# Neighbourhood attention: the scores of two heads in two neighbouring rows as four 64x64 blocks in the quarters of TensorE's array

## The reference, cut to what matters

```python
def neighbourhood_attention(q, k, v, rpb):
    """q,k,v: (B, T, H, dh); rpb: (H, 2*NA_KH-1, 2*NA_KW-1). Returns (B, T, H*dh)."""
    B, T, H, dh = q.shape
    R = T // GRID_W
    W = GRID_W
    KH = min(NA_KH, R)
    KW = NA_KW
    grid = lambda t: t.reshape(B, R, W, H, dh).transpose(0, 3, 1, 2, 4)
    qg, kg, vg = grid(q), grid(k), grid(v)
    rows = jnp.arange(R)
    row_start = jnp.clip(rows - KH // 2, 0, R - KH)
    row_idx = row_start[:, None] + jnp.arange(KH)[None, :]
    k_rows = kg[:, :, row_idx]
    v_rows = vg[:, :, row_idx]
    scores = jnp.einsum('bhrqd,bhrikd->bhrqik', qg, k_rows).astype(jnp.float32)
    scores = scores * (dh ** -0.5)
    dr_idx = row_idx - rows[:, None] + (NA_KH - 1)
    cols = jnp.arange(W)
    dc = cols[None, :] - cols[:, None]
    dc_idx = jnp.clip(dc, -(KW - 1), KW - 1) + (KW - 1)
    bias = rpb.astype(jnp.float32)[:, dr_idx[:, None, :, None], dc_idx[None, :, None, :]]
    col_start = jnp.clip(cols - KW // 2, 0, W - KW)
    in_win = (cols[None, :] >= col_start[:, None]) & (cols[None, :] < col_start[:, None] + KW)
    scores = jnp.where(in_win[None, None, None, :, None, :], scores + bias[None], -jnp.inf)
    p = jax.nn.softmax(scores.reshape(B, H, R, W, KH * W), axis=-1).reshape(B, H, R, W, KH, W)
    out = jnp.einsum('bhrqik,bhrikd->bhrqd', p.astype(v.dtype), v_rows)
    return out.transpose(0, 2, 3, 1, 4).reshape(B, T, H * dh)
```

## Time and profile before

| what | us |
|---|---|
| runs: median of 3 | 3050.95 |
| runs: lowest, highest | 3050.57, 3057.44 |
| the profiled execution's own time | 3060.26 |
| its span, first to last instruction | 3058.5 |
| neighbourhood stage in it, from the barrier's end to the next stage's first product | 2019.0 to 2164.6 |

### The profile page before, as it was taken

One profiled execution on the slowest core, in us unless ns is written; L12 is line 12 of the kernel. 1 busy time (PEld: TensorE's weight loads), 2 busy tenths in 40 slices (PEclk: granted clock), 3 DMA queues, 4 the chain that ended last, 5 costly groups with the idle time before them and its releaser, 6 DMA issues.

```text
span 3058.5 us, 30798 instructions
## 1 busy us (share of the span) xinstructions
PE 2889.4 (94%) x12002; PEld 1718.3 (56%) x12002; DVE 1169.8 (38%) x1999; ACT 629.4 (21%) x1351; POOL 724.3 (24%) x552
## 2 busy tenths in 40 slices
PE   7999998888988999999879999999999999999998
PEld 5886544888446666666534455557544444444443
DVE  6715766566122111111143135456543314133142
ACT  4001232222221222211222211157230000000001
POOL 3213556543111000000021000146521122111220
PEclk9999999999998999999989999999999999999999
DMA  8734494000237999999661100030201101111001
GB/s 265 224 54 52 96 228 136 1 28 29 107 143 282 397 424 428 426 426 395 250 231 55 56 0 15 14 107 1 90 31 52 55 28 41 42 55 47 36 28 55
DMA packets 180120, 415.12 MB, mean 136 GB/s; under 512 B 30644, under 2 KB 103796, under 8 KB 170872
## 3 DMA queue, kind: packets, MB, share of 16 engines
...
...
## 4 chain that ended last, share of the span: by engine, by line
PE 86%; DVE 6%; DMA 3%; issue 2%; ACT 1%; POOL 1%; SPq 0%; ACTq 0%; POOLq 0%; DVEq 0%
PE bank L3788 27%; PE bank L2554 9%; PE bank L2557 8%; PE bank L2984 5%; PE bank L1266 4%; PE bank L748 4%; PE bank L1946 4%; PE bank L3158 3%; PE bank L232 3%; PE bank L3497 2%; PE bank L3156 2%; PE bank L883 2%; PE bank L3487 2%; PE bank L1844 1%; PE bank L1841 1%
## 5 line engine op out<-in xcount | busy, mean ns | idle before, releaser
L3788 PE MATMUL bank<-w_ff,uT 128*128 128x512 f32 x640 | 276.0, 592 | 0.0
L3788 PE MATMUL bank<-hT,w_ff 128*128 128x512 f32 x512 | 225.1, 598 | 4.3 <-DVE hT L3591 4.3
L3788 PEld LDWEIGHTS bank<-w_ff,uT 128*128 128x128 f32 x640 | 121.7, 190 | 153.0 <-issue 153.0
L3911 DVE TENSOR_TENSOR x_out<-x_out,bank 128x512 f32<-128x512 f32 x140 | 94.5, 685 | 291.7 <-PE bank L3788 291.6
L2554 PE MATMUL bank<-e_w,e_xsT 128*128 128x256 f32 x832 | 184.4, 383 | 1.6 <-DVE e_xsT L2640 1.6
L2557 PE MATMUL bank<-e_w,e_xsT 128*64 128x256 f32 x1408 | 161.0, 389 | 17.1 <-issue 16.9
L2554 PEld LDWEIGHTS bank<-e_w,e_xsT 128*128 128x128 f32 x832 | 158.3, 191 | 32.5 <-issue 11.3
L2984 PE MATMUL bank<-w_gla,nT 128*128 128x512 f32 x384 | 167.5, 596 | 3.0 <-DMA w_gla<-in_w_in 1.7
L3788 PEld LDWEIGHTS bank<-hT,w_ff 128*128 128x128 f32 x512 | 97.9, 192 | 126.7 <-issue 126.7
L3788 PE MATMUL bank<-h_sum,w_ff 128*128 128x512 f32 x384 | 166.1, 592 | 0.0
L2557 PEld LDWEIGHTS bank<-e_w,e_xsT 128*64 128x64 f32 x1408 | 114.3, 140 | 67.5 <-issue 28.6
...
...
## 6 DMA issues: line engine op xcount, KB each, us to landing
...
w_ff<-in_w_ff SPq DMA_DIRECT2D x32, 1024.0 KB, 5.2
...
```

The costliest lines, as they stand in the source:

```text
L3788: t = pe.matmul(bank[:, :], still, moving, start=step in (0, 1, 3) and f == 0, stop=f == 3, skip_group_check=True)
L3911: v.tensor_tensor(dst, dst, k.bank[4 * ((ph + step) % 2) + g][:, :], ALU.add).then_inc(*s.added.up().inc)
```

## The change

The scores of one pair of heads are made for two neighbouring grid rows at once, 2r and 2r + 1, as four products of 64 features by 64 queries by 512 keys (`near_scores_tensor`, L3498). The features' half of the partitions picks the half of the array's rows; the half of the partitions that the output is written to picks the half of its columns. For the even row head 0's queries go to partitions 0 to 63 and head 1's to 64 to 127, for the odd row the other way round (`near_head`). So the four products lie in the four quarters of the array. Each row's scores are in a bank of their own, as before: banks p and p + 4 for the pair p.

For the odd row the heads stand turned, so the bias table is needed a second time with its halves swapped: `near.bias[1]`, loaded by two transfers of 64 partitions each behind the other transfers of that queue. VectorE waits for it ahead of its first instruction of the stage. It lies where the gated linear attention keeps a table, so its transfers wait until that one's last readers are done (`sums_made`).

The diagonal matrices go, with their copies and clears; the queries are scaled as ScalarE copies the projection. The transposed weights are written over the scores in `n_sc` instead of to `n_pT`, so the next reduce of a bank waits for the value products (`av_made`) instead of the transposes. The generators' order is by pairs (`NEAR_ORDER`: 0, 4, 1, 5, 2, 6, 3, 7), with other pauses.

The loads of SyncE's queue at the end of the projections, before and now. `n_bias` is the bias table, `w_ff` the weights of the next stage.

```diff
@@ -3067,7 +3067,7 @@
        "state_ready o_taken o_squared eps_added o_root o_ready o_turned mix_out zeroed")
 PAIRS = NAH // 2
 NEAR_RATE = 1.8
-Near = namedtuple("Near", "qkT val_even val_odd bias q2 sc pT st")
+Near = namedtuple("Near", "qkT val_even val_odd bias sc st")
 
 
...
@@ -3081,11 +3081,11 @@
 def gla(k, mix_s, mix_b, decay_s, decay_b, bias_rows, near):
 
     s = [k.on(GLA, way="_fwd"), k.on(GLA, way="_bwd")]
-    d = k.on("unit_made unit_out", "wv_got wqk_0 wqk_1 val_odd_got bias_got", way="_near")
+    d = k.on("unit_made unit_out", "wv_got wqk_0 wqk_1 val_odd_got bias_got bias_turned_got", way="_near")
...
-    near_loads(k, mix_s, d, wv, wqk, near, bias_rows)
+    near_loads(k, mix_s, s, d, wv, wqk, near, bias_rows)
...
@@ -3112,8 +3111,8 @@
 
     n_sets = lambda name, at, n, size: [k.at(f"n_{name}{j}", at + j * size * 4, P, size) for j in range(n)]
     return Near(k.at("n_qkT", U_AT + 48 * KB, P, 2 * PAIRS, T), k.at("n_val_even", U_AT + 80 * KB, P, NT, BANK), k.at("n_val_odd", N_AT, P, NT, BANK),
-                k.at("n_bias", N_AT + 16 * KB, P, PAIRS, (2 * KH - 1) * W), n_sets("q2", EARLY_AT, NSETS, P), n_sets("sc", U_AT + 96 * KB, NSETS, KH * W),
-                n_sets("pT", U_AT + 112 * KB, NSETS, KH * W), n_sets("st", EARLY_AT + 4 * KB, NSETS, 8))
+                [k.at(f"n_bias{j}", at, P, PAIRS, (2 * KH - 1) * W) for j, at in enumerate((N_AT + 16 * KB, U_AT + 96 * KB))],
+                n_sets("sc", U_AT + 112 * KB, NSETS, KH * W), n_sets("st", EARLY_AT + 4 * KB, NSETS, 8))
 
 
 def near_unit_of(u):
...
@@ -3134,9 +3133,13 @@
         sy.dma_start(wqk[at % 2][:, :, :], cols).then_inc(*(d.wqk_0, d.wqk_1)[at % 2].up().inc)
     sy.wait_ge(*d.unit_made(NT + 4 * PAIRS))
     sy.wait_ge(*d.unit_out(NT))
-    sy.dma_start(near.bias[:, :, :], bias_rows).then_inc(*d.bias_got.up().inc)
+    sy.dma_start(near.bias[0][:, :, :], bias_rows).then_inc(*d.bias_got.up().inc)
...
+    for way in gla_s:
+        sy.wait_ge(*way.sums_made(NT))
+    for lo in (0, W):
+        sy.dma_start(near.bias[1][W - lo:P - lo, :, :], bias_rows[lo:lo + W, :, :]).then_inc(*d.bias_turned_got.up().inc)
 
 
 def near_units_tensor(k, d, nT, wv, wqk):
@@ -3170,15 +3173,7 @@
             yield
         a.wait_ge(*d.unit_made(u + 1))
         dst = near.val_even[:, m, :] if m is not None else near.qkT[:, c, h * BANK:(h + 1) * BANK]
-        a.activation(dst, k.bank[6 + u % 2][:, :], ACT.Copy).then_inc(*d.unit_out.up().inc)
-
-
-def near_ready(k, decay_s, near):
-
-    g = k.nc.gpsimd
-    g.wait_ge(*decay_s.la_ready(2))
-    for n in range(NSETS):
-        g.memset(near.q2[n][:, :], 0.0).then_inc(*k.G.up().inc)
+        a.activation(dst, k.bank[6 + u % 2][:, :], ACT.Copy, scale=NAD ** -0.5 if m is None and c < PAIRS else 1.0).then_inc(*d.unit_out.up().inc)
 
 
 def gla_halves(n):
@@ -3400,18 +3395,29 @@
 def neighbourhood(k, d, b):
 
     k.nc.vector.wait_ge(*d.bias_got(1))
-    s = k.on("q_ready scored neg_max exp_ready sum_inverse weights_ready rows_turned pT_out av_made mix_out")
-    interleave(*(near_scalar(k, s, b, n) for n in range(NSETS)))
-    interleave(*(near_vector(k, s, b, n) for n in range(NSETS)))
-    interleave(*(near_gpsimd(k, s, b, n) for n in range(NSETS)))
-    interleave(*(near_tensor(k, s, d, b, n) for n in range(NSETS)))
+    k.nc.vector.wait_ge(*d.bias_turned_got(2))
+    s = k.on("scored neg_max exp_ready sum_inverse weights_ready rows_turned pT_out av_made mix_out")
+    interleave(*(near_scalar(k, s, b, n) for n in NEAR_ORDER))
+    interleave(*(near_vector(k, s, b, n) for n in NEAR_ORDER))
+    interleave(*(near_gpsimd(k, s, b, n) for n in NEAR_ORDER))
+    interleave(*(near_values_tensor(k, s, d, b, n) for n in NEAR_ORDER), *(near_scores_tensor(k, s, b, p) for p in range(PAIRS)))
     k.meet()
     k.retire(s + d)
 
 
+NEAR_ORDER = tuple(n for p in range(PAIRS) for n in (p, PAIRS + p))
+
+
+def near_start(n):
+
+
+    return pause(2 * (n % PAIRS) + n // PAIRS)
+
+
 def near_rows(n):
 
-    return [(r * NSETS + n, 2 * r + n // PAIRS, n % PAIRS) for r in range(ROWS // 2)]
+
+    return [(NSETS * r + NEAR_ORDER.index(n), 2 * r + n // PAIRS, n % PAIRS) for r in range(ROWS // 2)]
 
 
 def near_window(i):
@@ -3420,72 +3426,88 @@
     return lo, lo - i + KH - 1
 
 
+def near_head(n, h):
+
+
+    side = h if n < PAIRS else 1 - h
+    return slice(h * W, (h + 1) * W), slice(side * W, (side + 1) * W)
+
+
 def near_scalar(k, s, b, n):
 
-    a, q2, sc, st = k.nc.scalar, b.q2[n], b.sc[n], b.st[n]
-    yield from pause(n)
+    a, sc, st = k.nc.scalar, b.sc[n], b.st[n]
+    yield from near_start(n)
     for u, i, p in near_rows(n):
-        at = slice(i * W, (i + 1) * W)
-        if u >= NSETS:
-            a.wait_ge(*s.scored(u - NSETS + 1))
-        a.activation(q2[0:W, 0:W], b.qkT[0:W, p, at], ACT.Copy, scale=NAD ** -0.5).then_inc(*k.A.up().inc)
-        a.activation(q2[W:P, W:P], b.qkT[W:P, p, at], ACT.Copy, scale=NAD ** -0.5).then_inc(*s.q_ready.up().inc)
-        yield from pause(3)
+        yield from pause(4)
         a.wait_ge(*s.neg_max(u + 1))
         a.activation(sc[:, :], sc[:, :], ACT.Exp, scale=-1.0, bias=st[:, 0:1], accum_out=st[:, 1:2]).then_inc(*s.exp_ready.up().inc)
-        yield from pause(5)
+        yield from pause(4)
         a.wait_ge(*s.av_made(u + 1))
-        a.activation(b.qkT[0:W, p, at], k.bank[n][0:W, 0:W], ACT.Copy).then_inc(*k.A.up().inc)
-        a.activation(b.qkT[W:P, p, at], k.bank[n][W:P, W:P], ACT.Copy).then_inc(*s.mix_out.up().inc)
+        for h in range(2):
+            values, queries = near_head(n, h)
+            m = s.mix_out.up() if h else k.A.up()
+            a.activation(b.qkT[values, p, i * W:(i + 1) * W], k.bank[n][values, queries], ACT.Copy).then_inc(*m.inc)
 
 
 def near_vector(k, s, b, n):
 
     v, sc, st = k.nc.vector, b.sc[n], b.st[n]
-    yield from pause(n)
+    yield from near_start(n)
     for u, i, p in near_rows(n):
         _, dr = near_window(i)
-        yield from pause(2)
-        v.wait_ge(*s.scored(u + 1))
+        yield from pause(3)
+        v.wait_ge(*s.scored(u // 2 + 1))
         if u >= NSETS:
-            v.wait_ge(*s.rows_turned(u - NSETS + 1))
-        v.tensor_tensor_reduce(sc[:, :], k.bank[n][:, :], b.bias[:, p, dr * W:(dr + KH) * W], -1.0, -NEG, ALU.add, ALU.min, st[:, 0:1]).then_inc(*s.neg_max.up().inc)
+            v.wait_ge(*s.av_made(u - NSETS + 1))
+        v.tensor_tensor_reduce(sc[:, :], k.bank[n][:, :], b.bias[n // PAIRS][:, p, dr * W:(dr + KH) * W], -1.0, -NEG, ALU.add, ALU.min, st[:, 0:1]).then_inc(*s.neg_max.up().inc)
         yield from pause(2)
         v.wait_ge(*s.exp_ready(u + 1))
         v.reciprocal(st[:, 2:3], st[:, 1:2]).then_inc(*s.sum_inverse.up().inc)
         yield from pause(2)
         v.wait_ge(*s.rows_turned(u + 1))
-        if u >= NSETS:
-            v.wait_ge(*s.av_made(u - NSETS + 1))
-        v.tensor_copy(b.pT[n][:, :], k.bank[n][:, :]).then_inc(*s.pT_out.up().inc)
-        yield from pause(2)
+        v.tensor_copy(sc[:, :], k.bank[n][:, :]).then_inc(*s.pT_out.up().inc)
+        yield
 
 
...
+def near_scores_tensor(k, s, b, p):
+
+
+    pe = k.nc.tensor
+    yield from pause(2 * p)
+    for r in range(ROWS // 2):
+        yield from pause(2)
+        if r:
+            pe.wait_ge(*s.mix_out(NSETS * (r - 1) + 2 * p + 2))
+        for h in range(2):
+            for n in (p, PAIRS + p):
+                i = 2 * r + n // PAIRS
+                lo, _ = near_window(i)
+                features, queries = near_head(n, h)
+                t = pe.matmul(k.bank[n][queries, :], b.qkT[features, p, i * W:(i + 1) * W], b.qkT[features, PAIRS + p, lo * W:(lo + KH) * W], start=True, stop=True)
+        t.then_inc(*s.scored.up().inc)
+        yield from pause(6)
+
+
+def near_values_tensor(k, s, d, b, n):
 
     pe, bank = k.nc.tensor, k.bank[n]
-    yield from pause(n)
+    yield from near_start(n)
     for u, i, p in near_rows(n):
         lo, _ = near_window(i)
         val = b.val_odd if lo % 2 else b.val_even
-        yield
-        pe.wait_ge(*s.q_ready(u + 1))
-        if u >= NSETS:
-            pe.wait_ge(*s.mix_out(u - NSETS + 1))
-        pe.matmul(bank[:, :], b.q2[n][:, :], b.qkT[:, PAIRS + p, lo * W:(lo + KH) * W], start=True, stop=True).then_inc(*s.scored.up().inc)
-        yield from pause(4)
+        yield from pause(6)
         pe.wait_ge(*s.weights_ready(u + 1))
         pe.wait_ge(*s.neg_max(u + 1))
         transposes(k, bank, b.sc[n]).then_inc(*s.rows_turned.up().inc)
@@ -3494,9 +3516,8 @@
         if lo % 2:
             pe.wait_ge(*d.val_odd_got(2))
         for q in range(4):
-            t = pe.matmul(bank[:, 0:P], val[:, lo // 2 + q, p * P:(p + 1) * P], b.pT[n][:, q * P:(q + 1) * P], start=q == 0, stop=q == 3)
+            t = pe.matmul(bank[:, 0:P], val[:, lo // 2 + q, p * P:(p + 1) * P], b.sc[n][:, q * P:(q + 1) * P], start=q == 0, stop=q == 3)
         t.then_inc(*s.av_made.up().inc)
-        yield
 
 
 
```

10 lines of the change are left out of this document (4 added, 6 removed).

## The result

The changed kernel takes 3070.28 us (median of 5 runs, 3066.58 to 3071.63), the kernel before 3056.64 (5 runs, 3050.57 to 3057.75). The ratio is 1.0050, 95% interval 1.0036 to 1.0064: slower by about 14 us, with an interval that lies wholly above 1. The prediction said slower, at 3062.4 us in a range of 3053 to 3072; the measured time lies near the range's upper end.

A forecast was written before the change was run, and what follows sets the result against it. TensorE bounds the stage throughout: 121.8 us of work, 7.7 of waits, 1.2 stage end and 1.6 clock make 132.3 against 138.0; a start 17.1 us later nets +11.4, so 3062.4 us, range 3053 to 3072.

The forecast's parts named there:

- The quarters: Score products of a pair on TensorE: four quarters run at once, 1.22 us per pair with bubbles.
- The first rival: Score products: quarters run two at a time, 0.86 us more per pair, net +37, 3088 us; chance 0.11.
- The wait in a round: TensorE waits 1.03 us at bank 3's transposes and 0.1 elsewhere, 1.1 us per round of eight units.
- the second wait of 0.1 us: One more wait found in following a round's eight units on all four engines, 0.1 us, place not given.
- The second rival: Mid-stage: the wait behind the scores does not come, 7.7 us come back, 3054.6 us; chance 0.12.
- The second bias tile: Stage start: VectorE's first reduce waits for two new transfers landing at 2039.4; first transposes 17.1 us later.
- the third rival: Stage start: new transfers run at 341 GB/s and land at 2036.0, net +8.0, 3059 us; chance 0.12.
- the forecast's signs of being wrong: First reduce before 2036, a pair's scores over 1.5 us, or rounds of 15.6 us or less.
- The clock: TensorE's restart after standing idle ahead of the first transposes: lower clock at first, 1.6 us in the sum.
- The whole time: Whole kernel: net +11.4 us added to the median of the runs shown, 3050.95, gives 3062.4 us.

The follow-up runs named there:

- kinds: Against the changed kernel: turned bias tile early, VectorE's turn ordered reciprocals, copies, reduces, and TensorE's values ahead of the transposes; ratio 0.9959 to the kernel before.
- vorder: Against the changed kernel: turned bias tile early and VectorE's work of a turn ordered reciprocals, copies, reduces; ratio 0.9972 to the kernel before.
- early: Against the changed kernel: the turned bias tile's two transfers issued ahead of the wait for the last projections; ratio 0.9977 to the kernel before.
- the second experiment: Against the changed kernel: VectorE's reciprocal one turn earlier, ahead of the next unit's reduce, the turned bias tile still late; ratio 1.0051 to the kernel before.
- whole: Against the changed kernel: second bias tile by one transfer to all 128 partitions, same place in the queue, output wrong; one run, 3061.93 us.
- queue: Against the changed kernel: turned bias tile issued right behind the first bias tile, ahead of the odd values; one run, 3059.42 us.
- both: Against the changed kernel: turned bias tile issued early and VectorE's reciprocal one turn earlier; ratio 0.9976 to the kernel before.

## Why the prediction was right, point by point

The direction and the two terms behind it were right: a start 17.7 us later (17.1 forecast) and a stretch behind it 4.9 us shorter (5.7 forecast). By stage the net was +12.8 us for +11.4 forecast. Some of the closeness is luck, as points 1, 2 and 4 say.

1. **The quarters.** Forecast: 1.22 us per pair, four at once. Measured: 1.215 in kinds. The sum is closer than its parts: the forecast put 0.34 us of bubbles around 0.88 of products, and in kinds 1.02 us pass from the first start to the next whole product, and about 0.1 each lie in the transposes ahead (0.53 us for 0.44) and in the values behind (0.99 to 1.00 for 0.89). The first rival (two at a time, 0.86 us more per pair) is out by the start times. The rule that spoke for it, in the Trainium skill's page "TensorEngine Tiling (Array Packing)", section "Gotcha 1: PSUM Pressure", has row tiles keep out of one another's bank and leaves it to software to see to that; that they would go one after the other was the prediction's own reading. Here the two products of a bank come from different halves of the array's rows, go to different halves of the partitions, and start within 0.03 us of each other. The Trainium skill's page "PSUM — Partial Sum Buffer", section "PSUM bank collisions raise a hardware error", counts collisions by bank and quadrant, which agrees with these rows; but it also quotes the rule against row tiles in one bank, so it stood on both sides and not only against this rival.

2. **The wait in a round.** Forecast: 1.1 us per round, nearly all of it at the transposes of bank 3. Measured: rounds of 16.575 us (six rounds from the wait at 2051.64 to that at 2151.09; one of them from 2084.79 to 2101.37) against 15.50 without waits in kinds, so 1.08 us. The row of the earlier wait:

```profile
2084.79 0.66 PE L232 MATMUL bank<-consts,n_sc 128*128 128x128 f32 x4 [0.64 <-POOL n_sc L3480]
```

   The profile marks 0.64 us of it as idle. The rest doesn't show as idle time, because the ends of products are modelled: the values at 2099.57 need 0.89 us and 0.1 for a first record behind a wait, so the transposes at 2101.37 start 0.8 us late, where the forecast had 1.03. And those values show 1.16 us where the same products take 1.06 without a wait (2090.91 in kinds): they start 0.05 us behind the end of VectorE's copy (2098.83 + 0.69). This fits the second wait of 0.1 us in the forecast, which doesn't say where it had found it. The rest, under 0.2 us, lies in pieces of up to 0.06 us around the two waits; so here too the sum is closer than its parts. The second rival, a stage without that wait, is out. The cause was the order on VectorE, as argued: vorder changes that order alone against early, and the wait at bank 3 is gone. But that moving the reciprocal alone would mend it was a wrong guess of the second experiment. To be rid of all waits it took the order of two engines.

3. **The second bias tile.** Forecast: the wait is at VectorE's first reduce, at 20.6 us into the stage, and the first transposes 17.1 us late. Measured: 21.06 and 17.7. The second odd-value transfer of the changed kernel, its issue in the timeline and its time to landing in the DMA view:

```profile
2007.23 0.59 SPq L3138 DMA_DIRECT2D n_val_odd<-n_val_even  x1
```

```profile
n_val_odd<-n_val_even SPq DMA_DIRECT2D x1, 896.0 KB, 17.0
```

   The issue of the turned tile's second half, and the times to landing of the two halves, of which the longest is this one's:

```profile
2008.51 0.60 SPq L3142 DMA_DIRECT2D n_bias<-bias_rows  x1
DMA to landing us min/median/max: 20.8/23.1/25.3
```

   So the odd values are in at 2024.2 and the turned tile at 2033.8: the load took 9.6 us instead of 9.2, and the reduce starts 0.3 later, at 2034.08. The chain from there to the first transposes took 3.64 us for 3.55. That the form and not the source sets the rate, which decided against the third rival, is shown by whole, 5.7 us; that the place in the queue costs 10.7 us, by queue. The Trainium skill's page "SBUF — State Buffer", section "Door 1: The DMA port swizzle", gives half the partitions half the ports, and so about 218 GB/s at most; the turned tile's 1,966 KB in 9.6 us are 205 GB/s, which agrees.

   The third rival was mis-sized: with all partitions at a time the first reduce comes 5.7 us sooner and not 3.4, so the gain that it stood for was larger. The stage of that run is still 7.7 us above the one before.

   By its letter one of the forecast's signs of being wrong came true: the first reduce starts at 2034.08, before 2036. That time was meant in the profile of the kernel before, whose stage begins 6.0 us later; counted from the stage's start the sign lies at 17.0 us and the reduce at 21.06.

4. **The clock.** This is the term that was too small: 1.6 us in the sum, though the working beside it gives 1.5. The windows where TensorE starts again:

```profile
2036.00:2042.00 6.00, 4.28 (x18) 2.34 (x19) 2.81 (x10) 1.91 (x6) 4.70 (x3) 0.50 1.05 408
2042.00:2044.00 2.00, 2.00 (x20) 1.49 (x18) 1.62 (x5) 0.82 (x3) 1.24 (x1) 0.87 0.47 176
2044.00:2046.00 2.00, 2.00 (x21) 1.53 (x14) 1.11 (x4) 0.73 (x4) 1.53 (x2) 1.00 0.00 0
```

   Behind the idle stretch of 20.98 us TensorE works 4.28 us at 0.50 of full speed, the lower of its two levels (1.2 GHz), and 2 us at a mean of 0.87. That costs 4.28 x 0.5 + 2 x 0.13 = 2.4 us. The forecast had taken the 1.5 us from the stretch 2020 to 2024 of the kernel before. The 0.8 us more account for the difference between the forecast 132.3 us and the measured 133.1; the other terms are off by up to 0.3 us and cancel.

   But the long stand is not what sets this cost. In early TensorE is idle for 2.48 us ahead of its first transposes at 2023.70, and in the run both for 2.16 us ahead of those at 2017.11. Early's windows, and then that of the run both:

```profile
2024.00:2028.00 4.00, 4.00 (x19) 2.06 (x17) 1.65 (x5) 0.01 (x1) 2.76 (x2) 0.50 0.91 200
2028.00:2032.00 4.00, 4.00 (x30) 3.02 (x30) 2.72 (x8) 1.31 (x5) 2.51 (x2) 0.86 1.05 404
```

```profile
2016.00:2020.00 4.00, 2.45 (x17) 1.24 (x18) 2.12 (x7) 2.35 (x6) 3.91 (x3) 1.00 0.94 199
```

   In early the clock costs 0.3 x 0.5 + 4 x 0.5 + 4 x 0.14 = 2.7 us, and in the run both nothing. No run shows what decides between them. So it was right to give the clock a term, but its size was luck, and stage times of single profiles can differ by some 2.7 us from it alone; the orders are better compared by their rounds.

5. **The whole time.** The forecast of 3062.4 lies 7.9 us under the median of 3070.28. Most of that is the base: it was added to a median of three runs, 3050.95, and with two more runs the median of the same kernel is 3056.64. 5.7 us come from there, 1.4 from the stage, and 0.8 are left, less than the spread of the runs. The prediction gave its own mechanism a spread of about 3058 to 3068, which the measured median lies above; the range held it because it was wider.
